# Decays of pairs in the mixing stage: running sums stored as rows and read back to all partitions, clamped on GpSimd, in place of products on TensorE

## The reference

```
gc = jnp.cumsum(blocks(g), axis=-1)
causal = jnp.tril(jnp.ones((C, C), bool))
decay = jnp.exp(jnp.where(causal, gc[..., :, None] - gc[..., None, :], -jnp.inf))
L = jnp.where(strict, jnp.einsum('nbhcd,nbhjd->nbhcj', kb, kc) * decay, 0.0)
qk = jnp.einsum('nbhcd,nbhjd->nbhcj', qc, kc) * decay
```

## Time and profile before

| | us |
|---|---|
| median of 3 runs (lowest, highest) | 2845.32 (2842.64, 2845.61) |
| the profiled execution, in all | 2845.74 |
| its span in the trace | 2843.9 |
| TensorE busy, share of the span | 2340.7, 82% |
| VectorE busy | 1064.4, 37% |
| ScalarE busy | 698.8, 25% |
| GpSimd busy | 331.3, 12% |
| the changed product, L1453, 64 passes in 16 tiles, one pass | 0.593 |
| the spreading on GpSimd, L984, 16 times, one | 2.0 |
| TensorE's mean granted clock | 0.914 of full |

### The profile page before, as it was taken

One profiled execution on the slowest core, in us unless ns is written; L12 is line 12 of the kernel. 1 busy time (PEld: TensorE's weight loads), 2 busy tenths in 40 slices (PEclk: granted clock), 3 DMA queues, 4 the chain that ended last, 5 costly groups with the idle time before them and its releaser, 6 DMA issues. The chain is left out here.

```text
span 2843.9 us, 35628 instructions
## 1 busy us (share of the span) xinstructions
PE 2340.7 (82%) x13009; PEld 1330.3 (47%) x13009; DVE 1064.4 (37%) x1701; ACT 698.8 (25%) x1790; POOL 331.3 (12%) x369
## 2 busy tenths in 40 slices
PE   5999999999489999999999804434999999999940
PEld 3444444444276666666666502113444444444420
DVE  2515243341256565565565303635111111111127
ACT  2202121120145445445454201000111111111112
POOL 1010101001000110101100004001000000000036
PEclk9999999999689999999999955557999999999975
DMA  6062260704911121221311161046999999999846
GB/s 229 27 203 80 88 187 19 238 0 115 260 59 52 59 95 52 87 67 52 102 52 52 67 156 38 7 150 251 351 352 352 353 352 355 352 354 355 333 182 221
DMA packets 246182, 480.40 MB, mean 169 GB/s; under 512 B 46617, under 2 KB 157985, under 8 KB 221377
## 3 DMA queue, kind: packets, MB, share of 16 engines
q1 hardware_dynamic: 145761, 340.09, 34.3%
q10 hardware_dynamic: 86016, 86.58, 8.8%
q0 software_dynamic: 14272, 51.91, 5.2%
HBM read 351.66 MB, written 128.36 MB: 169 GB/s over the span
## 5 line engine op out<-in xcount | busy, mean ns | idle before, releaser
L680 PE MATMUL p_ps<-p_xt,p_w 128*128 128x512 f32 x1088 | 477.3, 598 | 0.7 <-issue 0.7
L2637 PE MATMUL p_ps<-p_w_arena,p_x_arena 128*128 128x512 f32 x1024 | 444.9, 593 | 0.0
L680 PEld LDWEIGHTS p_ps<-p_xt,p_w 128*128 128x128 f32 x1088 | 206.5, 192 | 259.6 <-issue 253.4
L2637 PEld LDWEIGHTS p_ps<-p_w_arena,p_x_arena 128*128 128x128 f32 x1024 | 195.0, 191 | 244.1 <-issue 244.1
L2653 PE MATMUL p_ps<-p_w_arena,p_y_arena 128*128 128x512 f32 x512 | 234.4, 601 | 20.5 <-ACT p_y_arena L2427 20.5
L1637 PE MATMUL p_ps<-p_w_out,p_mixt 128*128 128x512 f32 x512 | 237.2, 608 | 0.0
L2560 DVE SCALAR_TENSOR_TENSOR p_y_arena<-p_y_arena,p_ps 128x256 f32<-128x256 f32 x64 | 27.0, 421 | 462.2 <-ACT p_y_arena L2424 462.2
L2653 PEld LDWEIGHTS p_ps<-p_w_arena,p_y_arena 128*128 128x128 f32 x512 | 92.2, 190 | 120.3 <-issue 91.7
L689 PE MATMUL p_ps<-p_w,p_xt 128*128 128x144 f32 (+1 forms) x512 | 146.5, 439 | 0.0
L1637 PEld LDWEIGHTS p_ps<-p_w_out,p_mixt 128*128 128x128 f32 x512 | 93.6, 192 | 99.4 <-issue 97.4
L1257 DVE TENSOR_TENSOR p_inv<-p_inv,p_ps 128x256 f32<-128x256 f32 x160 | 66.0, 420 | 172.5 <-PE p_ps L1526 170.8
(11 more groups left out here) (388 smaller groups left out, 3186.4 us busy)
## 6 DMA issues: line engine op xcount, KB each, us to landing
p_w_arena<-in_w_exp_gate SPq DMA_DIRECT2D x64, 1024.0 KB, 9.8
p_w_arena<-in_w_exp_up SPq DMA_DIRECT2D x64, 1024.0 KB, 12.4
p_w_arena<-in_w_exp_down SPq DMA_DIRECT2D x64, 1024.0 KB, 11.9
s_y<-p_y_arena ACTq DMA_DIRECT2D x64, 512.0 KB, 9.1
s_y<-p_zero ACTq DMA_DIRECT2D x12, 2048.0 KB, 18.0
p_x<-in_x_prompt SPq DMA_DIRECT2D x32, 512.0 KB, 4.8
s_y<-p_zero ACTq DMA_DIRECT2D x4, 2560.0 KB, 16.0
p_w<-in_w_in SPq DMA_DIRECT2D x4, 2048.0 KB, 12.5
```

Of the source, the lines that this page charges most:

```text
L680: ins = mm(ps[:, job % 4, :], w[:, c, at:at + P], xt[s % 2][:, c, :], start=(c == 0), stop=(c == KC - 1))
L2637: t = mm(ps[:, 2 + b, :], xt[b][:, c, :], w_gu[bw][:, :, c, :], start=(c == 0), stop=(c == KC - 1))
```

## The change

The sums between two tokens are no longer summed by a product. The running sums, which TensorE makes for all tiles at once at the start anyway, are negated and copied out of PSUM by ScalarE (`gsum_neg`, tokens on partitions), transposed by TensorE so that a tile and head is a row, negated back (`gsum_rows`) and stored to a scratch tensor of 64 KB in memory. For each tile SyncE reads its eight rows of 128 values back, the same 4 KB to each of the 128 partitions (512 KB, `load_sums`). GpSimd adds, for each head, the negated running sum of the partition's own token and takes the smaller of that and 0, in place (`pair_sums`, eight instructions). ScalarE takes the exponentials from there. TensorE's two products per tile go, and so do the waits that kept banks 6 and 7 free for them; some of TensorE's other waits are replaced by narrower ones. `gsum` has two buffers.

The whole diff:

```diff
--- before.py
+++ after.py
@@ -836,7 +836,9 @@
         th = [sb(f"th{b}", [P, H, HD]) for b in two]
         x = sb("x", [P, D])
 
-        gt, dec = sb("gt", [P, H, P]), sb("dec", [P, H, P])
+        gsum = [sb(f"gsum{b}", [P, H, P]) for b in two]
+        dec = sb("dec", [P, H, P])
+        gsum_neg, gsum_rows = sb("gsum_neg", [P, NT, H]), sb("gsum_rows", [P, P])
         lt = [sb(f"lt{b}", [P, H, P]) for b in two]
         qkt = [sb(f"qkt{b}", [P, H, P]) for b in two]
         inv = sb("inv", [P, H, P])
@@ -862,6 +864,7 @@
         kq_in, kv_in, aq_in, ak_in, av_in, z_in = ([sem(f"{n}{b}_in") for b in two] for n in (
             "kq", "kv", "aq", "ak", "av", "z"))
         x_in = count("x_in", 16)
+        gsum_in = [sem(f"gsum{b}_in") for b in two]
         gt_ready, kd_ready, r8_ready, hr_ready = (count(n) for n in ("gt_ready", "kd_ready", "r8_ready", "hr_ready"))
         dec_ready, th_ready, vn1_ready, vn_ready, osq_ready = (count(n) for n in (
             "dec_ready", "th_ready", "vn1_ready", "vn_ready", "osq_ready"))
@@ -878,7 +881,7 @@
         masked, nmax_ready, den_ready, pt_vec, swa_mixed = count("masked", 2), count("nmax_ready"), count(
             "den_ready"), count("pt_vec"), count("swa_mixed")
         h_ready, hn_ready, hnt_vec = count("h_ready", 2), count("hn_ready"), count("hnt_vec")
-        scored, dsum_done, kkqk_done, qs_done = count("scored", 2), count("dsum_done", 2), count("kkqk_done"), count("qs_done")
+        scored, kkqk_done, qs_done = count("scored", 2), count("kkqk_done"), count("qs_done")
         inv0_turned, yc_done, x_done = count("inv0_turned", 2), count("yc_done", 2 * NL), count("x_done", 2 * NL)
         invt_turned = count("invt_turned", 2 * NL + 2)
         v1_done, lv_done, v_done, kdv_done, o_done = (count(n) for n in ("v1_done", "lv_done", "v_done", "kdv_done", "o_done"))
@@ -943,6 +946,10 @@
                 mix_ready.after(sp, t - 2)
                 load(zs[b][:].rearrange("p h d -> p (h d)"), rows(S["z"], t), z_in[b])
 
+            def load_sums(t):
+                dec_ready.after(sp, t - 2)
+                load(gsum[t % 2][:].rearrange("p h t -> p (h t)"), S["gsum"][t:t + 1].to_broadcast([P, H * P]), gsum_in[t % 2])
+
             load(gates, S["gb"][0:SEQ].rearrange("(n p) c -> p n c", p=P), on["gates_in"])
             load_keys(0)
             for dst, src in SMALL[:6]:
@@ -950,14 +957,20 @@
             load_values(0)
             for dst, src in SMALL[6:]:
                 load(dst, src, on["small_in"])
+            sp.wait_ge(on["rows_ready"], 1)
+            sp.dma_start(S["gsum"].rearrange("n (h p) -> (n h) p", p=P), gsum_rows[:]).then_inc(on["gsum_out"], 16)
             load_window(0)
             load_keys(1)
+            sp.wait_ge(on["gsum_out"], 16)
+            load_sums(0)
+            load_sums(1)
             load_values(1)
             for dst, src in WEIGHTS:
                 load(dst, src, on["weights_in"])
             load_window(1)
             load(x, rows(A["x_prompt"][0], 0), x_in.sem)
             for t in range(2, NT):
+                load_sums(t)
                 load_keys(t)
                 load_values(t)
                 h_ready.after(sp, t - 2)
@@ -979,10 +992,12 @@
             pool.wait_ge(on["small_in"], SMALL_IN)
             pool.wait_ge(on["gates_in"], 16)
 
-            def spread_gates(t):
-                dsum_done.after(pool, t - 1)
-                nc.gpsimd.tensor_tensor(gt[:], bc(gates[:, t, 0:H], [P, H, P], 2), bc(upto[:], [P, H, P], 1), ALU.mult
-                                        ).then_inc(gt_ready.sem, 1)
+            def pair_sums(t):
+                pool.wait_ge(gsum_in[t % 2], use(t))
+                for k in range(H):
+                    ins = nc.gpsimd.tensor_scalar(gsum[t % 2][:, k, :], gsum[t % 2][:, k, :], gsum_neg[:, t, k:k + 1], 0.0,
+                                                  ALU.add, ALU.min)
+                ins.then_inc(gt_ready.sem, 1)
 
             def key_decay(t):
                 b = t % 2
@@ -1004,12 +1019,13 @@
                 pool.wait_ge(on["hms_ready"], t + 1)
                 nc.gpsimd.tensor_tensor(hr[:], hms[:], half[:, 0:1], ALU.pow).then_inc(hr_ready.sem, 1)
 
-            spread_gates(0)
-            spread_gates(1)
+            pool.wait_ge(on["neg_ready"], 1)
+            pair_sums(0)
+            pair_sums(1)
             key_decay(0)
             for t in range(NT):
                 if t + 2 < NT:
-                    spread_gates(t + 2)
+                    pair_sums(t + 2)
                 output_roots(t)
                 if t + 1 < NT:
                     key_decay(t + 1)
@@ -1030,11 +1046,10 @@
             def pair_decays(t):
                 qkt_ready.after(act, t - 1)
                 lt_ready.after(act, t - 1)
-                for n in two:
-                    dsum_done.after(act, t, n + 1)
-                    for k in range(4):
-                        ins = nc.scalar.activation(dec[:, 4 * n + k, :], ps[:, 6 + n, k * P:(k + 1) * P], ACT.Exp,
-                                                   bias=gates[:, t, 2 * H + 4 * n + k:2 * H + 4 * n + k + 1])
+                gt_ready.after(act, t)
+                for k in range(H):
+                    ins = nc.scalar.activation(dec[:, k, :], gsum[t % 2][:, k, :], ACT.Exp,
+                                               bias=gates[:, t, 2 * H + k:2 * H + k + 1])
                 ins.then_inc(dec_ready.sem, 1)
 
             def lower_odd(t, n):
@@ -1139,6 +1154,9 @@
             act.wait_ge(on["gates_done"], 1)
             flat = "p t h -> p (t h)"
             sums = ps[:, 0, 0:3 * NT * H].rearrange("p (n c) -> p n c", n=3)
+            nc.scalar.mul(gsum_neg[:].rearrange(flat), sums[:, 0], -1.0).then_inc(on["neg_ready"], 1)
+            act.wait_ge(on["rows_turned"], 1)
+            nc.scalar.mul(gsum_rows[:], ps[:, 2, 0:P], -1.0).then_inc(on["rows_ready"], 1)
             nc.scalar.activation(e_up[:].rearrange(flat), sums[:, 0], ACT.Exp).then_inc(on["e_ready"], 1)
             act.wait_ge(on["left_ready"], 1)
             nc.scalar.activation(e_left[:], e_left[:], ACT.Exp).then_inc(on["e_ready"], 1)
@@ -1447,12 +1465,6 @@
         def _(pe):
             mm, tr = nc.tensor.matmul, nc.tensor.transpose
 
-            def pair_sums(t):
-                gt_ready.after(pe, t)
-                for n in two:
-                    mm(ps[:, 6 + n, :], after[:], gt[:, 4 * n:4 * n + 4, :].rearrange("p h t -> p (h t)"),
-                       start=True, stop=True).then_inc(dsum_done.sem, 1)
-
             def key_products(t):
                 b = t % 2
                 pe.wait_ge(kq_in[b], use(t))
@@ -1580,7 +1592,8 @@
                 if g == 0:
                     pe.wait_ge(aq_in[b], use(t))
                     pe.wait_ge(ak_in[b], use(t))
-                    dec_ready.after(pe, min(t + 1, NT - 1))
+                    h_ready.after(pe, t - 2)
+                    swa_mixed.after(pe, t - 1)
                     lg_ready.after(pe, t - 2)
                 else:
                     qs_read.after(pe, t)
@@ -1650,8 +1663,6 @@
                 hnt_vec.after(pe, t)
                 hnt_act.after(pe, t)
                 swa_mixed.after(pe, min(t + 1, NT - 1))
-                if t + 3 < NT:
-                    dec_ready.after(pe, t + 3)
                 for c in range(KC):
                     ins = mm(ps[:, 7, 0:NR], hnt[:, c, :], w_route[:, c, :], start=(c == 0), stop=(c == KC - 1))
                 ins.then_inc(lg_done.sem, 1)
@@ -1662,16 +1673,16 @@
                 ins = mm(ps[:, n % 2, n * NT * H:(n + 1) * NT * H].rearrange("p (t h) -> p t h", t=NT), m[:],
                          gates[:, :, 0:H], start=True, stop=True)
             ins.then_inc(on["gates_done"], 1)
+            pe.wait_ge(on["neg_ready"], 1)
+            tr(ps[:, 2, 0:P], gsum_neg[:].rearrange("p t h -> p (t h)"), ident[:]).then_inc(on["rows_turned"], 1)
             pe.wait_ge(on["e_ready"], 3)
-            pair_sums(0)
+            pe.wait_ge(on["rows_ready"], 1)
             key_products(0)
             first_inverse(0)
             for n in range(NL):
                 level_products(0, n)
                 level_turn(0, n)
                 level_update(0, n)
-            dec_ready.after(pe, 0)
-            pair_sums(1)
             level_turn(0, NL)
             pe.wait_ge(on["cleared"], 1)
             for t in range(NT):
@@ -1724,11 +1735,6 @@
                     level_products(t + 1, 3)
                     level_turn(t + 1, 3)
                     level_update(t + 1, 3)
-                if t + 2 < NT:
-                    if back:
-                        h_ready.after(pe, t - 1)
-                    swa_mixed.after(pe, t)
-                    pair_sums(t + 2)
                 if front:
                     level_products(t + 1, 4)
                     level_turn(t + 1, 4)
@@ -2675,6 +2681,7 @@
         "roots": dram("roots", (4, 4, 4, SEQ // 4)),
         "conv_s": dram("conv_s", (DB * (DT + CW - 1), CC)),
```

(1 more changed line is left out.)

## The result

| | before | after |
|---|---|---|
| median of 4 runs, us | 2845.47 | 3133.78 |
| lowest and highest | 2842.64, 2848.09 | 3132.63, 3134.46 |
| ratio to before, 95% interval | | 1.1013 (1.0994 to 1.1032) |
| span of the profiled execution | 2843.9 | 3132.3 |
| one steady iteration (mean of 12, from load of `x` to load of `x`) | 51.95 | 73.41 |

What follows compares the result with a forecast made beforehand. TensorE's own work was taken to set the pace. From 2845.7 us, 13 iterations of 16.3 us (12.7 chain plus 3.6 clock) add 212 and the start 7.5, giving 3065 us; range 3001 to 3106, widened to 2985 to 3118.

Steps and rivals of the forecast that it cites:

- SyncE's order and GpSimd's queue: Mixing loop: the sums' load is issued behind the wait for h_ready(t-1), GpSimd's three small jobs queue behind it; 13 iterations.
- The chain: Each held iteration: load, clamps, GpSimd's small jobs, layer_norm in series make hn's transposes 12.7 us later.
- the line between 64 and 512 columns: Clamps on GpSimd: 128 columns priced between 453 and 1494 ns, giving 602 ns each, 4.9 us for eight with gaps.
- the slope at small sizes: Clamps on GpSimd, upper end: from 0.20 us at 8 columns to 453 ns at 64, 0.75 us each, 6.2 us with gaps.
- The clock: Behind TensorE's stand of 14 us: about 7.2 us at half clock lose 3.6 us an iteration, 0.9 to 4.5.
- The start: Start of the stage: lower(0) 10.1 us later, two credits of 1.3 us against it, together +7.5 us.
- The credits of 1.3 us: Ahead of the loop and in iteration 0: each removed product of sums gives back 1.3 us against the later start.
- Cover: TensorE, each tile: removed products save 1.92 us but covered VectorE's update of inv; 0.6 us of wait leaves 1.3 us net.
- Rival 2: Mixing loop: the sums are there in time, nothing is late, so the kernel is faster, 2836 us; chance 0.06.
- Rival 1: Behind TensorE's stand: GpSimd is held but the clock comes back at once, 3018 us; chance 0.15.
- the signs named for the trace: Profile after: GpSimd's longest wait at the clamps, over 50 us; layer_norm about 13 us late; iterations 16 us longer.

Runs made afterwards that it cites:

- e1_early: Changed kernel with the load of the sums of tile t+1 issued ahead of SyncE's wait for h_ready(t-2), one iteration earlier; 2844.7 us, 1.0002 of before.
- e2_clamps_last: Changed kernel with GpSimd's pair_sums(t + 2) moved behind layer_root(t - 1), SyncE's order unaltered; 3061.6 us, 1.0773 of before.
- e9_hold22: Kernel before, nothing of the change, with 22 more GpSimd instructions, each waited for, in layer_root in iterations 1 to 13; 3139.8 us, 1.1031 of before.
- e5_fill17: Changed kernel with 17 products of 512 columns, results not used, ahead of the transposes of hn in the 13 held iterations; 3034.5 us, 1.0661 of before.
- e10_dense_behind: Changed kernel with 8 unused products of 512 columns right behind the transposes of hn in the 13 held iterations; 3157.8 us, 1.1103 of before.
- e8_hold13: Kernel before, nothing of the change, with 13 more GpSimd instructions, each waited for, in layer_root in iterations 1 to 13; 3034.4 us, 1.0661 of before.
- e3_fill: Changed kernel with 15 products of 512 columns, results not used, ahead of the transposes of hn in the 13 held iterations; 3105.0 us, 1.0909 of before.
- e7_hold7: Kernel before, nothing of the change, with 7 more GpSimd instructions, each waited for, in layer_root in iterations 1 to 13; 2972.5 us, 1.0443 of before.

## Why the prediction was wrong, by its steps

- **SyncE's order and GpSimd's queue: right.** The load stands behind `h_ready(t-1)`, and `output_roots`, `key_decay` and `layer_root` stand behind it; 13 iterations. Shown by e1_early and e2_clamps_last; that a late `hr` alone makes such a loss, by e9_hold22.
- **The chain, 12.7 us: measured 14.2 in the mean, 14.5 in the iteration shown, 14.1 by e5_fill17.** In the iteration shown: issue 3.4 (3.5 forecast); landing to the first clamp 7.1 (5.9 forecast, above its end of 6.6); the clamps 5.54 (4.9); the small jobs 3.9 (3.8); `layer_norm` 1.96. A single clamp is 0.71 us, against 0.60 from the line between 64 and 512 columns and 0.75 from the slope at small sizes. The figure that I had worked out from the Trainium skill's "GPSIMD Engine Reference", Performance versus the Vector engine, an estimated 2.4 us for eight, is less than half of what was measured.
- **The clock, 3.6 us, at most 4.5: this is the step that failed.** It is 7.2 us by the trace and 7.4 by e5_fill17, outside its bounds. The step read "about 7 us at the lower level" off the end of the stage, where 512-column products of the projection follow, and used it for a place where transposes and products of 64 to 256 columns follow; there it lasts 14.8 to 17.7 us. e10_dense_behind puts dense products there, and the clock is back after 4.0 to 5.4. Of the 69 us that the forecast missed, the clock's 3.6 to 3.8 us an iteration are 47 to 49, the chain's 1.4 to 1.5, inside its bounds, 18 to 20, and the start 4.5. Why the length differs where the same small work follows (e8_hold13) stays open.
- **The start, +7.5 us with all of iteration 0: measured 12.0.** `lower(0)` is 13.1 us late, not 10.1: the first clamp began 8.2 us after its load was issued, where the prediction has 5.4, and eight took 5.5 us, not 4.9. That it ran at 782.37, just where the prediction had put it, is luck, since the stage began 3.0 us sooner in that execution. The credits of 1.3 us for two removed products came out as 1.1 us together.
- **Cover: partly right.** Freed of the hold, TensorE is ready 1.5 us sooner, against 1.3 forecast, but an iteration gains only 0.8 us, since `hn` becomes the bound.
- Rival 2 (the sums are there in time) was put at 2836 us, and e1_early measured 2844.7: the gain of an iteration and the cost of the start were each misjudged, to the same side. Rival 1 (clock back at once) has its price in e5_fill17: 3034, and not 3018.

Of the signs named for the trace those of the mechanism were all there: the longest of GpSimd's waits 64.8 us, the DMA its releaser, `layer_norm` 15 us late, 13 times. Those of size were off: the lower clock lasted twice as long and more, the clamps took 0.71 us each and began 7.1 us after their load, and an iteration was 21.5 us longer, not 16.

## What to carry to other kernels

A load that feeds an in-order engine has two queues to clear: ask behind which wait it is issued, and which jobs of its consumer's engine stand behind it; a nearly idle engine can still hold the bound one by what is queued behind its wait. Here moving one load ahead of one wait was worth 288 us. Price a stand of TensorE by its length and by the clock behind it, and take the second from a place where the same kind of work follows: 4 us of stand cost 10.7 us here, and the changed kernel's lower clock lasted 15 to 18 us before small products and 4 to 5.4 us with dense ones put there.

## What the runs showed of the hardware that was not expected

- Behind dense products, pauses of 1.8 to 4.5 us ahead of the transposes went with a fall of the clock in 11 of 13 iterations (e3_fill), pauses of 0.1 to 1.6 us with none in 13 (e5_fill17). The length of the pause alone doesn't decide: the clock fell behind one of 1.9 us and held behind one of 2.1. What does wasn't tested further.
- The mean loss by the clock hardly depends on the length of the stand: 6.4 us behind 4.2 us, 5.5 behind 9.1, 6.7 behind 16.3. Behind a stand of 2.6 us, in one iteration of e7_hold7, there was none.
- VectorE's `layer_norm` took 3.59 us where GpSimd's spreading of the gates (1.90 us) ran beside it, and 1.97 us where it didn't (e7_hold7, e8_hold13, e9_hold22). In the kernel before the two overlap by 0.44 us, and it takes 2.06.
- GpSimd's tensor_scalar on 128 x 128 fp32 with a column operand took 0.71 us; eight spend 5.5 us on 1024 columns, for which one tensor_tensor took 2.0. The 64 us more that GpSimd was busy in e1_early stood in no chain that bound the kernel: its iterations were shorter than before.
- The broadcast of a stored 4 KB row to 128 partitions took 6.6 us to land (median; 9.1 where it was issued last of its burst, in e1_early):

```profile
p_gsum<-s_gsum SPq DMA_DIRECT2D x13, 512.0 KB, 6.6
```
